# The rotation of the retention's queries and keys: from VectorE's share of the dilated attention to GpSimd beside it

## What is computed

```python
def rope(x, pos):
    half = x.shape[-1] // 2
    ...
    x1, x2 = xf[..., :half], xf[..., half:]
    return jnp.concatenate([x1 * cos - x2 * sin, x1 * sin + x2 * cos], axis=-1)

q_d = hfirst(rope(heads(p['d_q'], D_HEADS), pos))
d = {'q': q_d,
     'k': hfirst(rope(heads(p['d_k'], D_HEADS), pos)) * HEAD_DIM ** -0.5,
     ...
```

## Time and profile before

| | us |
|---|---|
| median of three runs | 3034.73 (3034.09 to 3038.99) |
| the profiled execution, its own time | 3030.9 |
| its span, first to last instruction | 3029.2 |
| TensorE busy | 2889.0 (95%) |
| VectorE busy | 2127.4 (70%) |
| ScalarE busy | 1008.5 (33%) |
| GpSimd busy | 811.9 (27%) |

### The profile page before, as it was taken

How to read it: one execution, slowest core, us unless ns; L and a number is a source line. 1 busy time by engine, 2 the same in 40 slices (tenths; PEclk the granted TensorE clock), 3 DMA queues, 4 the chain that set the end, 5 groups by cost and what they waited for, 6 DMA issues and landing times.

```text
span 3029.2 us, 61547 instructions
## 1 busy us (share of the span) xinstructions
PE 2889.0 (95%) x23632; PEld 2671.8 (88%) x23648; DVE 2127.4 (70%) x3715; ACT 1008.5 (33%) x1719; POOL 811.9 (27%) x882
## 2 busy tenths in 40 slices
PE   7999999998999999999989999999899999999996
PEld 6799985767899999999978999767688999999996
DVE  5699986797464444598848999766965544447887
ACT  3422123243233333343433221223323333334334
POOL 4252510000023333244341543000100332233532
PEclk9999999999999999999999999999999999999998
DMA  7343435243112222332143543443310222224323
GB/s 271 106 150 126 148 117 224 87 133 114 42 51 77 85 85 85 113 137 92 56 139 102 155 146 128 188 186 97 119 65 28 85 85 80 75 71 157 101 79 106
DMA packets 139283, 340.26 MB, mean 112 GB/s; under 512 B 20661, under 2 KB 72006, under 8 KB 135030
## 3 DMA queue, kind: packets, MB, share of 16 engines
q1 hardware_dynamic: 90050, 177.19, 16.4%
q0 software_dynamic: 33088, 102.84, 11.0%
q10 hardware_dynamic: 15844, 56.20, 5.3%
HBM read 266.11 MB, written 74.53 MB: 112 GB/s over the span
## 4 chain that ended last, share of the span: by engine, by line
PE 81%; DVE 10%; issue 3%; ACT 2%; DVEq 2%; DMA 1%; POOL 0%; SPq 0%; ACTq 0%; POOLq 0%
PE PS L1610 25%; PE PS L1175 15%; PE PS L1643 12%; PE PS L1189 5%; PE PS L1548 3%; PE PS L1020 2%; PE PS L1519 2%; PE PS L1521 2%; PE PS L1520 2%; PE PS L1099 2%; PE PS L1412 2%; PE PS L1121 1%; PE PS L1140 1%; DVE U L2693 1%; DVE U L2517 1%
## 5 line engine op out<-in xcount | busy, mean ns | idle before, releaser
L2429 DVE TENSOR_TENSOR RGR<-WS,RGR 128x512 fp32r<-128x512 f32 (+2 forms) x504 | 349.0, 693 | 284.3 <-ACT RGR L1704 283.6
L1704 ACT ACTIVATE RGR<-WS 128x512 fp32r<-128x512 f32 (+3 forms) x510 | 292.8, 576 | 525.9 <-PE PS L1610 251.4
L751 POOL TENSOR_TENSOR WS<-WS 128x512 f32<-128x512 f32 (+2 forms) x288 | 393.1, 1375 | 178.9 <-DMA WS<-wjobs 85.3
L706 POOL DMA_DIRECT2D WS<-wjobs x176 | 94.7, 538 | 964.3 <-DVE RGR L2429 606.9
L2542 DVE TENSOR_SCALAR_CACHE_REDUCE U<-U,smu 128x384 bf16<-128x384 f32 (+5 forms) x396 | 348.5, 943 | 6.6 <-issue 0.9
L1610 PE MATMUL PS<-XBR,RGR 128*128 128x264 f32 x2560 | 341.0, 284 | 1.8 <-DVE U L2440 1.1
L1704 ACT ACTIVATE U<-PS 128x528 f32<-128x528 f32 (+12 forms) x326 | 158.6, 498 | 528.0 <-PE PS L1610 229.3
L1610 PEld LDWEIGHTS PS<-XBR,RGR 128*128 128x128 f32 x2560 | 323.5, 188 | 2.6 <-issue 1.4
L1643 PE MATMUL PS<-XBR,RGR 128*128 128x264 f32 x1760 | 242.2, 284 | 0.0
L736 POOL TENSOR_TENSOR WSR<-WS,HNHR 128x1024 fp32r<-128x1024 f32 x50 | 121.6, 2438 | 412.4 <-ACT HNHR L1704 412.4
L1643 PEld LDWEIGHTS PS<-XBR,RGR 128*128 128x128 f32 x1760 | 225.6, 188 | 0.0
(11 more groups left out here) (375 smaller groups left out, 5582.0 us busy)
## 6 DMA issues: line engine op xcount, KB each, us to landing
WS<-wjobs POOLq DMA_DIRECT2D x113, 512.0 KB, 3.8
WS<-wjobs ACTq DMA_DIRECT2D x50, 512.0 KB, 4.5
hmid<-U SPq DMA_DIRECT2D x44, 528.0 KB, 2.7
WS<-wjobs POOLq DMA_DIRECT2D x48, 384.0 KB, 3.4
Hn<-ckT SPq DMA_DIRECT2D x16, 896.0 KB, 10.8
U<-hmid SPq DMA_DIRECT2D x16, 792.0 KB, 6.9
U<-kT_pool SPq DMA_DIRECT2D x160, 64.0 KB, 2.0
xres<-U SPq DMA_DIRECT2D x2, 4224.0 KB, 16.3
```

Of the source, the lines that this page charges most:

```text
L706: pool.dma_start(slot(j % NJOBS, n), wjobs[bass.ds(L * NJOBS + j, 1), :, 0:n].rearrange("a p n -> (a p) n")).then_inc(w_in[j % NJOBS % NSL ...
L751: pool.tensor_tensor(out=plain(p, to, g), in0=plain(p, a, g), in1=plain(p, b, g), op=op).then_inc(fw_sum, 1)
L1704: return act.activation(out, in_, ACT.Copy)
L2429: tt(out=lo, in0=plain(p, i, g), in1=hi.bitcast(F32), op=ALU.subtract).then_inc(wp_lo, 1)
```

## The change

The twelve instructions leave VectorE and become twelve plain tensor operations of GpSimd, placed in its program between the loop over the projection steps and the wait for the end of the attention. The keys' factor moves into the scale of their projection's eviction, so the copy of the keys in `dtok` is already scaled. A new semaphore, `pd_turned`, takes the place of the second increment of `g_ready` for TensorE, ScalarE and SyncE, and VectorE's `decay_d` waits for it where it drained before.

```diff
-        pd_in, pd_rot, pd_val, pd_gate = (sem(f"pd_{q}") for q in ("in", "rot", "val", "gate"))
+        pd_in, pd_rot, pd_val, pd_gate, pd_turned = (sem(f"pd_{q}") for q in ("in", "rot", "val", "gate", "turned"))
...
         for r in range(6):
-            STEPS_P.append(("T", (J_D + r,), ((0, 1, 2, 1, 2, 0)[r],), dtok[:, r, :], ACT.Copy, 1.0))
+            STEPS_P.append(("T", (J_D + r,), ((0, 1, 2, 1, 2, 0)[r],), dtok[:, r, :], ACT.Copy,
+                            E ** -0.5 if 2 <= r < 4 else 1.0))
...
-        ROPE = [0] * 6 + [1, 2, 3, 4, 5, 6, 7, 8, 9, 10, 11, 12, 12]
...
+                def rope():
+
+                    pool.wait_ge(tab_in, 32)
+                    pool.wait_ge(pd_in, 16)
+                    for r in range(4):
+                        pool.tensor_tensor(out=dr[:, r, :], in0=dr[:, r, :], in1=U[:, COS:COS + TT], op=ALU.mult)
+                    pool.wait_ge(pd_rot, 64)
+                    for r in range(4):
+                        pool.tensor_tensor(out=zd[:, r, :], in0=zd[:, r, :], in1=U[:, SIN_T:SIN_T + TT], op=ALU.mult)
+                    pool.drain()
+                    for r in range(4):
+                        i = pool.tensor_tensor(out=zd[:, r, :], in0=zd[:, r, :], in1=dr[:, r, :], op=ALU.add)
+                    i.then_inc(pd_turned, 1)
...
                         (keys if call == "k" else values)(n, places)
+                rope()
                 for j in range(J_OUT + NSLOT, J_GU + NSLOT):
...
                 sp.wait_ge(as_v, 2 * NB)
-                sp.wait_ge(g_ready, 2)
+                sp.wait_ge(pd_turned, 1)
...
-                pe.wait_ge(g_ready, k + 1)
+                pe.wait_ge(*((pd_turned, 1) if k else (g_ready, 1)))
...
-                act.wait_ge(g_ready, 2)
+                act.wait_ge(pd_turned, 1)
...
-                    for n in range(ROPE[s], ROPE[s + 1]) if k == 1 else ():
-                        if n == 0:
-                            v.wait_ge(tab_in, 32)
-                            v.wait_ge(pd_in, 16)
-                        elif n == 4:
-                            v.wait_ge(pd_rot, 64)
-                        elif n == 8:
-                            v.drain()
-                        rope(n // 4, n % 4)
...
-            def rope(part, r):
-
-                cos, sin = U[:, COS:COS + TT], U[:, SIN_T:SIN_T + TT]
-                f = 1.0 if r < 2 else E ** -0.5
-                if part == 0:
-                    stt(out=dr[:, r, :], in0=dr[:, r, :], scalar=f, in1=cos, op0=ALU.mult, op1=ALU.mult)
-                elif part == 1:
-                    stt(out=zd[:, r, :], in0=zd[:, r, :], scalar=f, in1=sin, op0=ALU.mult, op1=ALU.mult)
-                else:
-                    i = tt(out=zd[:, r, :], in0=zd[:, r, :], in1=dr[:, r, :], op=ALU.add)
-                    if r == 3:
-                        i.then_inc(g_ready, 1)
-
             def decay_d():
 
-                v.drain()
+                v.wait_ge(pd_turned, 1)
```

## The result

| | before | after |
|---|---|---|
| median, us | 3034.6 (20 runs, 3029.9 to 3043.8) | 3042.7 (20 runs, 3037.8 to 3062.2) |
| ratio, with its 95% interval | | 1.0031 [1.0021, 1.0042] |
| profiled execution, its span | 3029.2 | 3051.5 |
| VectorE busy | 2127.4 | 2106.3 |
| GpSimd busy | 811.9 | 872.6 |

The kernel became slower: the ratio makes it 9.4 us (6.4 to 12.7; the two medians lie 8.1 apart), against a forecast of 3.5 us less. VectorE is relieved of 21 us, and none of that is seen in the time.

The account below looks back on a forecast made before the run. VectorE and TensorE were both taken as full in the attention's large steps, TensorE setting the pace without the rotation. 1.11 + 0.65 = 1.76 us a layer, 3.5 in both: 3034.7 - 3.5 = 3031.2 us; range 3024 to 3038.

Parts of the forecast that it names:

- GpSimd's twelve operations: Rotation on GpSimd during the attention: 2.43 us each, 29.2 us in all, ending near 646 us, hidden before 679.9 us.
- No disturbance of VectorE in the attention: VectorE's attention instructions, with at most one SBUF input, were to lose nothing beside GpSimd's operations.
- The third: Rival in the attention: GpSimd's operations hold `L2676` and `L2699`, at most 29.2 us a layer, 3050.7 to 3065 us; chance 0.07.
- the fourth rival: Rotation on GpSimd doesn't hide, over 5.2 us an operation; at 6 us each, 3053 us; chance 0.02.
- The gain of the attention: Shorter TensorE waits in `attend(1)`: 1.11 + 0.65 = 1.76 us a layer, 3.5 us in both.
- with 1.16 us less in front they go. I count 1.11.: First four TensorE waits in the attention, for VectorE's copy or ScalarE's exponential, were to vanish: 1.11 us a layer.
- The tail: Last five TensorE waits of the attention, mostly behind `L2699`, were to shrink by 0.65 us a layer.
- The clock behind the attention: Granted clock right after the attention's end: a denser end may keep it up or lose it, 2.7 us either way.
- the first rival: More comes back in the attention: all nine TensorE waits go, 10.0 us, 3024.7 us; chance 0.20.
- Second, the gain is given back at once: Rival behind the attention: GpSimd's cast and subtractions fall on `decay_d`, making it 5.9 us later; 3035.1 us; chance 0.12.
- The second rival's sum: GpSimd's split falling on `decay_d` behind the attention: net 2.1 and 1.8 us by layer, +3.9, 3035.1 us.
- The delay that `L2763` has today goes: Credit behind the attention against the later `decay_d`: 1.9 us in layer one, 4.1 us in layer two.

Follow-up runs that it names:

- e1: The changed kernel, with GpSimd's split of two mixer rows also waiting until VectorE's `decay_d` is done; 3028.1 us median, ratio 0.9983.
- e3: The changed kernel, with a semaphore in place of the drain inside GpSimd's rotation; 3029.2 us, ratio 0.9987.
- e5: The changed kernel with the split waiting for `decay_d`, plus one more GpSimd drain near the layer's start; ran once, under the profiler, 3039.2 us.
- e6: The changed kernel, with seven more filler products on TensorE ahead of the product that waits 3.3 us; 3041.2 us, ratio 1.0024.
- e7: The changed kernel, with the eight instructions of `decay_d` also issued by GpSimd, behind the rotation and a drain; 3027.6 us, ratio 0.9977.
- e2: The kernel before, with one more drain on GpSimd ahead of its wait for the attention's end; 3042.0 us, ratio 1.0039.
- e4: The kernel before, with eleven of VectorE's twelve rotation instructions left out and only the last addition kept; 3030.8 us, ratio 0.9986.
- e8: The kernel before, rotation still on VectorE, with GpSimd draining before the attention's end and its split waiting for `decay_d`; 3034.0 us, ratio 0.9994.

## Why the prediction was wrong

**GpSimd's twelve operations:** right. Four take 9.61 us, 2.40 each, against 2.43 taken; done by 669.3 us even with 9.4 us more in the middle, which the working had allowed for. The attention of this execution starts 12.45 us later than that of before, so that is 656.9 on the scale of the prediction, which had 646 and 9.4 on top.

**No disturbance of VectorE in the attention:** right. All instructions of the biasing step in after (ns min/median/max); the largest form took 1231 ns at most before:

```profile
L2691 DVE CUSTOM_DVE_ANT_0 U<-PS,U x128: 281/756/1225, 445.8 to 2183.2; 128x128 f32<-128x128 f32 x16, 128x256 f32<-128x256 f32 x16, 128x384 f32<-128x384 f32 x16, 128x512 f32<-128x512 f32 x16
```

The third and the fourth rival fell with these two. The Trainium skill, page "SBUF — State Buffer", section "Who interferes with whom", had this right on both counts: one SBUF input does not contend, as here, and two do, as `decay_d` does. Its rule that the one which comes second waits in full roughly fits VectorE's side: `decay_d` grew by 6.21 us beside casts and subtractions that take 2 x (1.06 + 2.43) = 6.98 us undisturbed. GpSimd's side grew too, by 2.59 us, to 1.99 + 3.31 + 1.06 + 3.21.

**The gain of the attention:** wrong, 3.5 us forecast, 1.05 measured at equal starts. The step that failed is "with 1.16 us less in front they go. I count 1.11." Of the four waits none went: they are 0.26, 0.20, 0.22 and, at 676.39 us, 0.33 us in after. That VectorE was busy without a gap had made me take its last instruction for the cause. The copy that releases the last two starts when TensorE's own transposes are done (VectorE waits 0.82 and 0.93 us for them). The copy that releases the first two follows the biasing instructions without a gap, but these now wait for TensorE's scores:

```profile
640.67 1.09 DVE L2691 CUSTOM_DVE_ANT_0 U<-PS,U 128x896 f32<-128x896 f32 x1 [1.01 <-PE PS L1114]
```

So most of the rotation's 1.16 us became idle time of VectorE, and the copies come as late behind TensorE's work as before. The working has a slip at the same place: TensorE's need for a step of 5.92 us was put at "about 5.6 us", from 0.12 us open in 15; that makes 5.87, so a step had 0.05 us to lose and not 0.3. The tail was nearer: 1.09 became 0.92 and 0.76 became 0.66, 0.27 us where 0.65 was forecast; 0.60 stayed. A comparison of the two profiled layers would have hidden this, since it shows 1.83 us, close to the 1.76 forecast, of which 1.2 are the clock at the attention's start.

**The clock behind the attention:** named under the first rival, and it came. In all twelve layers profiled with the rotation on GpSimd (after, e1, e3, e5, e6, e7) `L1330`'s 48 products take 2.80 us; without it, five of eight (before, e2, e4, e8) take about 5. The 2.7 us priced for it are what the table shows, 26.5 against 23.8. Why a denser VectorE, or e4's single addition, should lead to it isn't settled.

**The choice between the cases:** here the forecast failed. "Second, the gain is given back at once" described what happened, down to `decay_d`'s price (5.9 us said, 5.31 measured), and was given 0.12. The step that failed here put a term at nothing: "GpSimd's next work, the split of the mixer rows, waits for the attention's end anyhow, so nothing is queued behind the new waits." The split does wait for the attention's end, but the rotation's drain had used up the 9.4 us that kept its subtractions off `decay_d`; the runs show 3.31 us of waiting and 2.87 of slower products in each layer for it. The reason to see it stood in the rows ahead of the prediction: 9.40 us "<-issue" in front of the second instruction of GpSimd's stretch, with a `drain` written between the two, and a change that puts another drain ahead of it.

**The second rival's sum:** +3.9 us said for the retention, where the table has 3.52 + 5.44 = 9.0. Three credits and costs were mis-sized. (a) "The delay that `L2763` has today goes" took 1.9 and 4.1 us off. But in layer one `L2763` was not on the path: VectorE waited for TensorE behind it (1.44 us at `L2775` in before, 5.52 us in after), and nothing came back. In layer two 0.67 us did (the wait at `L1468`, 2.32 in before and 1.65 after), and behind it `L1503` ran at the lower level, 1.69 us longer. (b) What VectorE's slack takes up, "1.89 us" in layer one and none in layer two, is 1.78 in both, as e1's rows show, and TensorE has 1.12 more. (c) The clock behind the new wait wasn't priced: a wait of 3.31 us is followed by 2.87 us of slower products, in each layer. By these the retention of a layer costs 3.31 + 2.87 = 6.2 us against an undisturbed one, or 6.2 - 0.67 = 5.5 against before's second layer, where 5.44 were measured.

**The range:** 3038 was its upper end, from that sum. With the retention's 9.0 in place of 3.9 it would have stood at 3034.7 - 3.5 + 9.0 = 3040.2; with the measured attention (-1.05) and last column (-0.36 + 1.33) as well it is 3034.7 + 8.9 = 3043.6. These are the measured stretches put in, not a test of them. Of the 12.4 us between the forecast's -3.5 and +8.9 the attention makes 2.4, the retention 9.0 and the last column 1.0.

## What to carry to other kernels

An idle stretch that the profile puts down to nothing ("issue") is part of the schedule: here a drain of 9.4 us kept GpSimd's two-input operations off VectorE's two-input operations by accident, and any edit that pays that drain earlier removes the cover. When work moves to an engine, follow that engine to its next work too, and ask what starts earlier; if it must not, write the wait down (here one `wait_ge`, worth 14.6 us between the medians of after and e1). Before crediting an engine's saving, look at who releases it: VectorE, busy without a gap, gave 0.5 us a layer in the attention for 13.9 us of work taken away, because TensorE set the pace.

## What was not expected of the hardware

- A `drain` on GpSimd can take 9.4 us with nothing to wait for that the profile shows, and the next ones 0.14 to 0.17 us. It took 9.40 us behind one cast (before), behind eight operations (after) and behind thirteen (e3), 9.60 in e5. It is paid once between the projections of a layer and the split, wherever the first drain stands; a drain ahead of the projections doesn't pay it (e5). In that stretch GpSimd issues the page loads (`L691`) and weight loads; whether the drain waits for something of theirs wasn't tried and stays open.
- Of VectorE and GpSimd, both with two SBUF inputs, both got slower: VectorE's eight instructions 5.03 to 11.24 us, GpSimd's subtraction 2.43 to 3.3. A cast, with one SBUF input, went from 1.06 to 1.99 beside it, and `decay_d` from 5.03 to 5.93 when only a cast lay beside it. Which of the two started first shows in the cast: 1.99 us where `decay_d` was 0.15 us ahead of it (both layers of after, e3 and e6), 1.06 us where the cast was 0.02 or 0.03 us ahead (before, e2, e4).
- A wait of TensorE of 3.3 us cost nearly as much again in the clock behind it (2.87 us); where the fillers had shortened the first wait, a second of 2.49 us still had slow products behind it, 1.52 for 1.09 us and 3.15 for 1.97.
